# Attention outputs: copying the reciprocals instead of the sums, and splitting the result on Pool

## What is computed

```
e = exp(logits - m)
p = e / (sum(e) + exp(sink - m))       # the sink in C alone
out = p @ v                            # then out @ w_out
```

## Time and profile before

| | us |
|---|---|
| median of 3 runs | 2841.89 (2839.76 to 2844.17) |
| the profiled execution | 2836.89 |
| its span, first to last instruction | 2835.1 |
| attention, even layer | about 396 to 758 |
| attention, odd layer | about 1801 to 1943 |

### The profile page before, as it was taken

The page is one execution under the profiler, slowest core; times in us unless marked ns, Lnnn a source line. Parts: engine busy times, 40 slices in busy tenths (PEclk is TensorE's granted clock), DMA queues, the critical chain, the costliest instruction groups (busy, mean ns, idle before and its releaser), DMA issues. The chain is left out here.

```text
span 2835.1 us, 41848 instructions
## 1 busy us (share of the span) xinstructions
PE 2667.9 (94%) x16695; PEld 2440.0 (86%) x16695; DVE 1310.5 (46%) x2840; ACT 940.8 (33%) x2129; POOL 813.5 (29%) x862
## 2 busy tenths in 40 slices
PE   5989987788899999999999989898999999999999
PEld 5766765566799999999999978678999999999999
DVE  5458999998333222222222366784422222222224
ACT  5355425576623111111111241695221111111110
POOL 5588800000214222222222167312322222222220
PEclk9999988899999999999999999999999999999999
DMA  5212331101202111111111113201111111111111
GB/s 160 58 49 64 107 136 37 40 29 54 93 2 74 45 45 45 45 45 45 45 45 45 31 48 98 75 29 45 30 46 45 45 45 45 45 45 45 45 45 64
DMA packets 90961, 154.75 MB, mean 55 GB/s; under 512 B 12240, under 2 KB 27472, under 8 KB 90640
## 3 DMA queue, kind: packets, MB, share of 16 engines
q1 hardware_dynamic: 72832, 128.74, 14.6%
q10 hardware_dynamic: 17936, 23.35, 2.3%
HBM read 127.13 MB, written 24.92 MB: 54 GB/s over the span
## 5 line engine op out<-in xcount | busy, mean ns | idle before, releaser
L829 PE MATMUL s_banks<-act_hi,ring_hi 128*128 128x352 f32 (+1 forms) x2496 | 817.5, 328 | 5.8 <-DVE act_lo L1923 4.5
L831 PE MATMUL s_banks<-act_hi,ring_lo 128*128 128x352 f32 (+1 forms) x2496 | 813.7, 326 | 0.0
L830 PE MATMUL s_banks<-act_lo,ring_hi 128*128 128x352 f32 (+1 forms) x2496 | 813.2, 326 | 0.0
L1579 POOL TENSOR_TENSOR ring_lo<-raw,ring_hi 128x512 fp32r<-128x512 f32 x264 | 336.6, 1306 | 1151.2 <-ACT ring_hi L1405 1149.7
L829 PEld LDWEIGHTS s_banks<-act_hi,ring_hi 128*128 128x128 f32 x2496 | 468.6, 188 | 8.4 <-DVE act_lo L1923 4.9
L830 PEld LDWEIGHTS s_banks<-act_lo,ring_hi 128*128 128x128 f32 x2496 | 470.0, 188 | 0.8
L831 PEld LDWEIGHTS s_banks<-act_hi,ring_lo 128*128 128x128 f32 x2496 | 468.3, 188 | 0.0
L1974 DVE TENSOR_TENSOR silu_out<-silu_out,s_banks 128x384 f32<-128x384 f32 x132 | 70.3, 533 | 829.6 <-ACT silu_out L1418 829.6
L1985 DVE TENSOR_TENSOR xT<-xT,bank 128x352 f32<-128x352 f32 (+1 forms) x480 | 253.3, 532 | 191.7 <-PE bank L831 191.7
L1418 ACT ACTIVATE silu_out<-s_banks 128x384 f32<-128x384 f32 x132 | 62.7, 475 | 783.5 <-PE s_banks L831 783.5
L829 PE MATMUL bank<-hT_hi,ring_hi 128*128 128x352 f32 (+1 forms) x960 | 313.6, 327 | 0.0
(11 more groups left out here) (164 smaller groups left out, 3769.6 us busy)
## 6 DMA issues: line engine op xcount, KB each, us to landing
raw<-in_w_up SPq DMA_DIRECT2D x176, 256.0 KB, 3.1
raw<-in_w_down SPq DMA_DIRECT2D x88, 256.0 KB, 2.9
raw<-in_w_even SPq DMA_DIRECT2D x40, 256.0 KB, 2.7
raw<-in_w_out SPq DMA_DIRECT2D x32, 256.0 KB, 2.9
scratch_cq<-p_out ACTq DMA_DIRECT2D x18, 256.0 KB, 2.0
q_tok<-scratch_cq SPq DMA_DIRECT2D x9, 512.0 KB, 3.4
xT<-in_xT SPq DMA_DIRECT2D x8, 544.0 KB, 5.1
out_yT<-xT SPq DMA_DIRECT2D x8, 544.0 KB, 2.7
```

The source lines that it names most:

```text
L829: pe.matmul(out, w_hi, x_hi, start=first, stop=False)
L830: pe.matmul(out, w_hi, x_lo, start=False, stop=False)
L831: return pe.matmul(out, w_lo, x_hi, start=False, stop=last)
L1579: pool.tensor_tensor(ring_lo[:, sl + k, :], raw[:, k % 4, :], ring_hi[:, sl + k, :].bitcast(F32), ALU.subtract).then_inc(lo_done, 1)
```

## The change

The reciprocals are now transposed ahead of q, k and the probabilities of an iteration, directly behind `times_values` (list `outs` in place of `late`, and in front of `early` in the order of bank 7). ScalarE copies them from bank 7 into `y` (`copy_inv`, `inv_copy`), before everything else in its iteration. VectorE multiplies `y` by bank 6. So bank 7 is free after ScalarE's copy, and bank 6 after VectorE's multiply. `out_hi` and `out_lo` leave ScalarE and VectorE: Pool copies `y` to `act_hi` and subtracts for `act_lo`, behind its spreading of the reciprocals.

```diff
@@ Plan
         for s in self.early:
-            self.uses += self.early[s] + self.late[s]
+            self.uses += self.outs[s] + self.early[s]
@@ pe_attention, transposes(use)
                     if before[0] == "o":
-                        pe.wait_ge(s.o_scaled, plan.count("o", before))
+                        pe.wait_ge(s.inv_copy, plan.count("o", before))
@@ pe_attention, times_values(n)
                 if i % job.og_steps == 0 and g:
-                    pe.wait_ge(s.o_copy, g)
+                    pe.wait_ge(s.o_scaled, g)
@@ pe_attention, the loop
-                for use in plan.early[n]:
+                for use in plan.outs[n] + plan.early[n]:
                     transposes(use)
                 if 0 <= n - plan.tr_lag < n_steps:
                     transpose_probs(n - plan.tr_lag)
-                for use in plan.late[n]:
-                    transposes(use)
@@ act_attention
-            def copy_out(g):
-
-                act.wait_ge(s.pv_mm, plan.last_step(g) + 1)
+            def copy_inv(g):
+
+                act.wait_ge(s.tr_mm, plan.use_no[("o",) + plan.groups[g]] + 1)
                 if g:
                     act.wait_ge(s.o_lo, g)
-                act.activation(b_["y"][:, :], bank(6), ACT.Copy).then_inc(s.o_copy, 1)
-
-            def out_hi(g):
...
-                act.wait_ge(s.o_scaled, g + 1)
-                src = b_["y"][:, :].rearrange("p (a b) -> p a b", a=4)[:, :, 0:c1 - c0]
-                act.activation(act_hi[:, k0:k0 + 4, c0:c1], src, ACT.Copy).then_inc(s.o_hi, 1)
+                act.activation(b_["y"][:, :], bank(7), ACT.Copy).then_inc(s.inv_copy, 1)
@@ act_attention, the loop
             for n in range(n_steps + plan.tail):
+                for use in plan.outs[n]:
+                    copy_inv(plan.group_no[use[1:]])
                 for use in plan.early[n]:
                     bank7(use)
-                if n and plan.late[n - 1]:
-                    out_hi(plan.group_no[plan.late[n - 1][0][1:]])
                 if 0 <= n - plan.tr_lag < n_steps:
                     probs_out(n - plan.tr_lag)
-                for use in plan.late[n]:
-                    copy_out(plan.group_no[use[1:]])
@@ pool_attention
                 pool.tensor_copy(b_["inv"][:, :, :], inv).then_inc(s.inv_wide, 1)
...
+                pool.wait_ge(s.o_scaled, g + 1)
+                pool.tensor_copy(act_hi[:, k0:k0 + 4, c0:c1], y).then_inc(s.o_hi, 1)
+                pool.wait_ge(s.o_hi, g + 1)
+                pool.tensor_tensor(act_lo[:, k0:k0 + 4, c0:c1], y, act_hi[:, k0:k0 + 4, c0:c1].bitcast(F32),
+                                   ALU.subtract).then_inc(s.o_lo, 1)
@@ dve_attention
             def scale_out(g):
 
-                dve.wait_ge(s.o_copy, g + 1)
-                dve.wait_ge(s.tr_mm, plan.use_no[("o",) + plan.groups[g]] + 1)
+                dve.wait_ge(s.pv_mm, plan.last_step(g) + 1)
+                dve.wait_ge(s.inv_copy, g + 1)
                 y = b_["y"][:, :]
-                dve.tensor_tensor(y, y, bank(7), ALU.mult).then_inc(s.o_scaled, 1)
+                dve.tensor_tensor(y, y, bank(6), ALU.mult).then_inc(s.o_scaled, 1)
@@ dve_attention, the loop
-                if n and plan.late[n - 1]:
-                    out_lo(plan.group_no[plan.late[n - 1][0][1:]])
```

More of the change, by code:

```diff
@@ L161, in __init__ @@
         self.early = {s: [] for s in range(-1, len(self.steps) + self.tail)}
-        self.late = {s: [] for s in self.early}
+        self.outs = {s: [] for s in self.early}
         self.early[-1] = self.bank_uses(0, "q") + self.bank_uses(0, "k")
@@ L174, in __init__ @@
             for i in range(job.steps // job.og_steps):
-                self.late[f + (i + 1) * job.og_steps - 1 + pv_lag] += [("o", j, i)]
+                self.outs[f + (i + 1) * job.og_steps - 1 + pv_lag] += [("o", j, i)]
         self.groups = [(j, i) for j, job in enumerate(jobs) for i in range(job.steps // job.og_steps)]
@@ L502, in __init__ @@
                 self.pv_mm = sem(f"pv_mm{n}")
-                self.o_copy = sem(f"o_copy{n}")
+                self.inv_copy = sem(f"inv_copy{n}")
                 self.inv = sem(f"inv{n}")
@@ L1590, in pool_attention @@
                 pool.tensor_copy(b_["inv"][:, :, :], inv).then_inc(s.inv_wide, 1)
+                job = plan.jobs[j]
+                c0, c1 = tile_cols(job.t)
+                if job.t == 0:
+                    c1 = SAMPLE
+                k0 = 4 if job.kind == "B" else 4 * i
+                y = b_["y"][:, :].rearrange("p (a b) -> p a b", a=4)[:, :, 0:c1 - c0]
+                pool.wait_ge(s.o_scaled, g + 1)
[3 more added lines that the diff above has]
+                                   ALU.subtract).then_inc(s.o_lo, 1)
         def pool_norm_rstd(pool, n, c):
@@ L1912, in mask_logits @@
                                              ALU.add, ALU.min, neg_max[:, n % 6, x:x + 1]).then_inc(s.logit, 1)
[L1914 to L1924, removed]
             for i in range(3):
@@ L1938, in dve_attention @@
                     mask_logits(n)
-                if n + 1 in plan.late:
-                    for use in plan.late[n + 1]:
+                if n + 1 in plan.outs:
+                    for use in plan.outs[n + 1]:
                         invert_sums(plan.group_no[use[1:]])
-                for use in plan.late[n]:
+                for use in plan.outs[n]:
                     scale_out(plan.group_no[use[1:]])
```

## The result

The changed kernel took 2856.61 us (median of 11 runs, 2846.39 to 2862.31), the kernel before on the same chip 2839.11 us (11 runs). The ratio is 1.0055, with a 95% interval of 1.0044 to 1.0066: 15.6 us slower (12.5 to 18.7). The ratio is formed over all runs; the two medians lie 17.5 us apart, and where this text gives a difference it goes by the ratio. Measured once more it was 1.0036 (1.0020 to 1.0051), so 10.2 us slower (5.7 to 14.5). The forecast was 9.3 us slower, with an upper end of the range 19 us above the 2841.9 that it started from.

A forecast was written before the change was run, and what follows sets the result against it. VectorE (92% busy) was taken to bound the even attention, ScalarE (96%) the odd. The terms +8.4 - 0.8 - 1 + 2.7 = +9.3 us gave a profiled 2846.2 and a median of 2851.2 us, range 2841 to 2861.

The forecast's parts named there:

- The round trip over bank 7: Odd layer: q and k wait for ScalarE's copy of the reciprocals; period 16.5 us against 15.38, +8.4 over jobs 1 to 7.
- -0.8: Odd layer, job 8: no q or k behind it, so it keeps ScalarE's gain of twice 0.52, less a little.
- ScalarE's saved slots: Odd layer: ScalarE loses `out_hi`, a slot of 0.52 us per group, 1.04 us a job.
- The even order: Even layer: `scale_out` no longer waits behind probability copies, 9.0 us gained in 15 groups; later probabilities cost VectorE 5.2.
- The even split: Even layer: `out_lo` gone gives VectorE 8.5 us; collisions of its tiny updates with Pool's pair cost 10 (0 to 20).
- Rival A: Even layer: Pool's pair meets no VectorE updates; even stage -9, in all +1.3 us, 2843; chance 0.20.
- VectorE's -9.0, -8.5 and +5.2: Even layer: waits before `scale_out` gone, `out_lo` gone, longer waits for probabilities; TensorE can follow only part.
- The layer ends: Output projection: reciprocals' transposes come later and Pool does both halves before weight splits; twice 1.35, +2.7 us.
- Rival C: Odd layer: both round trips in full, +2.0 a job, even collision at its upper end; +20 us, 2862; chance 0.18.
- Rival B: Odd layer gains: reciprocals copied before ScalarE's exponentials end, 16 groups give -8.3; in all -15 us, 2827; chance 0.07.

The follow-up runs named there:

- e7: Whole change in the odd layer alone, with q and k of the next job transposed one step later each, against the kernel before: ratio 1.0006, +1.7 us.
- e6: Whole change in the odd layer alone, even layer as before, against the kernel before: ratio 1.0030, +8.5 us.
- e4: Odd layer alone with both halves made by Pool in the old order, against the kernel before: ratio 1.0001, +0.3 us.
- e1: New order in both layers, halves still made by ScalarE and VectorE, against the kernel before: ratio 1.0022, +6.2 us.
- e5: New order in the even layer alone, halves still made by ScalarE and VectorE, against the kernel before: ratio 0.9981, -5.4 us.
- e3: Whole change in the even layer alone, odd layer as before, against the kernel before: ratio 1.0014, +4.0 us.
- e9: As e3, but Pool's pair covers one column of each 128 in the first 15 groups; against the kernel before: ratio 0.9956, -12.5 us.
- e2: Both halves made by Pool in both layers, old order kept, against the kernel before: ratio 1.0035, +9.9 us.

## Why the prediction was right, and where it was wrong

The direction, the size within its range (+15.6 and +10.2 for +9.3), and the layer that pays most were right. In the even layer two errors partly cancelled: the order gained more than was summed and the split cost far more. That the total came so near is in part luck. By its own steps:

- **The round trip over bank 7.** Walked to a period of 16.5 us; it is 16.36 or 16.37 in all three profiles that have the whole change in the odd layer. The waits stand where the walk put them: TensorE for the reciprocals' copy (0.69 and 0.93), ScalarE for k and q (0.42 and 0.74), VectorE's mask for the logits. e7 is the proof of the cause. The walk gives +1.1 a job, entered as +1.2; +0.98 was measured. The term with its -0.8 and the layer end made 9.0 us for the odd layer; e6 measured 8.5.
- **ScalarE's saved slots** were counted in full in the walk (1.04 us a job). With the old order they are worth 0.43 (e4), since TensorE is next; with the new one 16.92 - 16.36 = 0.56 (e1 against the change).
- **The even order.** Summed as -9.0 and +5.2, so -3.8; e5 measured -5.4 (-8.2 to -2.6), with its end of the layer.
- **The even split: the term that was mis-sized.** Summed as -8.5 for `act_lo` and +10 for the collisions, +1.5 in all; e3 less e5 measured +9.4. The first term was near (e9 less e5 is -7.1). The second was too small: lengthened instructions of 7.5 us, less than the 10 reckoned, cost 16.5 by the runs of e9 and 13.6 by its trace. I priced a collision at the length that it adds on VectorE. In the step of e2 above it came with a longer wait of TensorE for the maxima, a stretch at the lower clock and a wait of VectorE for TensorE; that these make up the difference in the whole stage is argued, not shown. Rival A, no collisions, is excluded for the changed kernel: e9 is what it described, with updates at 0.17 us and 16.5 us under e3. Its -9 for the even stage was too little, as e9 is at -12.5. (The prediction puts the forecast without collisions 10 us lower in one place and, in rival A, 8.)
- **VectorE's -9.0, -8.5 and +5.2.** Together -12.3 without collisions, of which TensorE was said to be able to follow only part. e9, where only these are left, has an even stage 10.8 us under that of before (362.6 to 351.8), a later end of the layer included: these terms were right, and TensorE did follow. Waits removed from VectorE came back in part as its wait for the probabilities (20.8 us before, 28.8 in e9, 33.2 with the collisions), in kind as the +5.2 said.
- **The layer ends.** Reckoned +1.35 each. The first added piece came 0.97 us later behind the last multiply, and TensorE's wait for `act_lo` grew by 1.27 us. TensorE's waits for the `ring_lo` splits (0.25 and 0.45 us before) are gone in exchange, so less of it counts than I said.
- **Rival C** (both round trips in full, period +2.0, clock falls) had the period wrong, and in the rest of the odd layer the clock stayed at 1.00; the clock's part is in the first odd jobs of one profile. In the even layer its clock was 0.89, and 0.93 in e9, while four profiles of the code of before have 0.88 to 0.91, so that little can be read from it. Where C was near is the even layer: with the collision at its upper end it had +4 there and +1.35 for the end, and e3 is +4.0 where the forecast had +0.35. **Rival B** is excluded by the order of ScalarE's queue, as written: the copy started when the exponentials had ended.

The prediction cites a rule from the Trainium skill's "SBUF — State Buffer", section "Who interferes with whom". The trace agrees: the `kth` update, with two SBUF inputs, took 1.13 us beside Pool's subtraction, and with the short pieces of e9 no `kth` update took more than 0.17. The section also says that issue order decides who blocks, and that shows here the other way round: beside a scan of the top-k search that had started first, Pool's `act_hi` took 2.01 us in place of 0.61.

```profile
511.86 1.75 DVE L1745 TENSOR_TENSOR_SCAN mask_cum<-mask_flags 128x768 f32<-128x768 bf16 x1
...
512.01 2.01 POOL L1583 CAST act_hi<-y 128x512 fp32r<-128x512 f32 x1 [5.96 <-DVE y L1864]
```

## What to carry to other kernels

Before an instruction that frees a shared buffer is put ahead of another user of it, walk the loop once: copy, next user, and everything queued behind that user; a second use in the same step cost about 1 us a job here, and moving it to a step of its own gave it back. Work taken to an idle engine is not free where it holds up the bound engine's small instructions (1.09 us for 0.17 here), and its price is what the loop of engines makes of the delay (13.6 to 16.5 us for 7.5 us here), not the delay. And measure the parts of a change apart: this one held a gain of 5.4 us (the even order) under losses of 9.4 (the even split) and 8.5 (the odd layer), and its good part alone beats both kernels.

## What the runs showed of the hardware that I had not expected

- After a wait of TensorE of 2.37 us in place of 1.45, 16 matmuls took 1.78 us for 1.09, and the next multiply came 2.2 us later for a 0.93 us collision. But after the same wait of 1.97 us eight matmuls took 2.40 us in one kernel and 1.30 in another.
- `enough`, a VectorE instruction with one input tile of 128x2, was held up by Pool's subtraction as the two-input updates were (1.09 us for 0.17), and Pool's copy by VectorE's scan (2.01 us for 0.61).
- The same code of the even attention took 362.3 to 366.0 us in four profiles. The odd one took 147.8 to 148.0 in five, with a granted clock of 0.71 to 0.74 over its first 20 us, and 150.5 in one, with 0.50. So a single profile can't tell 3 us in a stage from nothing.
